# A hybrid mLSTM, window and neighbourhood attention step on one core: the final norm's path to the output, and the place of two instructions in the attention schedules

## What is computed

```python
def _rmsnorm(x, w):
    xf = x.astype(jnp.float32)
    y = xf * lax.rsqrt(jnp.mean(xf * xf, axis=-1, keepdims=True) + NORM_EPS)
    return (y * w.astype(jnp.float32)).astype(x.dtype)
...
    y_prompt = _rmsnorm(xc, final_norm_w)
    y_sample = _rmsnorm(xl, final_norm_w)
```

## Time and profile before

| what | value |
|---|---|
| device time, median of 3 runs | 1920.52 us (1920.36 to 1920.54) |
| the profiled execution's own time | 1920.54 us |
| its span, first to last instruction | 1918.7 us |
| busy: PE / DVE / ACT / POOL | 1862.4 / 1269.0 / 931.1 / 270.2 us |
| mean granted TensorE clock | 0.99 of full speed |
| DMA | 412.99 MB, 215 GB/s over the span |

### The profile page before, as it was taken

The page is one execution under the profiler, slowest core; times in us unless marked ns, Lnnn a source line. Parts: engine busy times, 40 slices in busy tenths (PEclk is TensorE's granted clock), DMA queues, the critical chain, the costliest instruction groups (busy, mean ns, idle before and its releaser), DMA issues.

```text
span 1918.7 us, 32356 instructions
## 1 busy us (share of the span) xinstructions
PE 1862.4 (97%) x13828; PEld 1660.9 (87%) x13828; DVE 1269.0 (66%) x1737; ACT 931.1 (49%) x1373; POOL 270.2 (14%) x198
## 2 busy tenths in 40 slices
PE   5999999999999999999999999999999999989998
PEld 2999777798999867999977689998998777889998
DVE  3854576666786566787555678857655776658874
ACT  2753344544564354555344455645543445436552
POOL 2100121002111112111011221101100220021111
PEclk8999999999999999999999999999999999989999
DMA  9555346866655757655574775456654447634552
GB/s 369 191 224 190 139 154 241 299 230 266 233 182 194 275 214 293 242 212 198 180 303 174 289 281 217 177 199 242 227 191 154 156 173 280 247 143 176 187 187 77
DMA packets 65823, 412.99 MB, mean 215 GB/s; under 512 B 11744, under 2 KB 12048, under 8 KB 17424
## 3 DMA queue, kind: packets, MB, share of 16 engines
q1 hardware_dynamic: 54288, 392.98, 54.9%
q10 hardware_dynamic: 11392, 17.95, 2.7%
HBM read 400.10 MB, written 10.76 MB: 214 GB/s over the span
## 4 chain that ended last, share of the span: by engine, by line
PE 88%; DVE 5%; POOL 2%; ACT 2%; issue 2%; DMA 1%; POOLq 0%; DVEq 0%; ACTq 0%; SPq 0%
PE ps L537 15%; PE ps L538 14%; PE ps L539 14%; PE ps L554 9%; PE ps L588 6%; PE ps L590 6%; PE ps L589 6%; PE ps L570 4%; PE ps L601 3%; PE ps L821 1%; DMA raw<-in_stream 1%; DVE spl_lo L454 1%; PE ps L805 1%; POOL hf L2192 1%; ACT Ea L1365 1%
## 5 line engine op out<-in xcount | busy, mean ns | idle before, releaser
L454 DVE TENSOR_TENSOR spl_lo<-raw,spl_hi 128x1024 fp32r<-128x1024 f32 x556 | 727.9, 1341 | 266.6 <-ACT spl_hi L443 265.8
L443 ACT ACTIVATE spl_hi<-raw 128x1024 fp32r<-128x1024 f32 x556 | 566.6, 1054 | 310.6 <-PE ps L590 163.2
L537 PE MATMUL ps<-H_hi,spl_hi 128*128 128x256 f32 x1920 | 549.4, 286 | 11.7 <-DVE H_lo L1619 10.1
L538 PE MATMUL ps<-H_lo,spl_hi 128*128 128x256 f32 x1920 | 545.4, 284 | 0.0
L539 PE MATMUL ps<-H_hi,spl_lo 128*128 128x256 f32 x1920 | 545.2, 284 | 0.0
L537 PEld LDWEIGHTS ps<-H_hi,spl_hi 128*128 128x128 f32 x1920 | 370.5, 193 | 32.3 <-issue 32.2
L538 PEld LDWEIGHTS ps<-H_lo,spl_hi 128*128 128x128 f32 x1920 | 370.7, 193 | 0.1
L539 PEld LDWEIGHTS ps<-H_hi,spl_lo 128*128 128x128 f32 x1920 | 370.6, 193 | 0.0
L588 PE MATMUL ps<-G_hi,spl_hi 128*128 128x256 f32 x704 | 199.2, 283 | 0.0
L589 PE MATMUL ps<-G_lo,spl_hi 128*128 128x256 f32 x704 | 199.2, 283 | 0.0
L590 PE MATMUL ps<-G_hi,spl_lo 128*128 128x256 f32 x704 | 199.2, 283 | 0.0
(11 more groups left out here) (241 smaller groups left out, 2778.2 us busy)
## 6 DMA issues: line engine op xcount, KB each, us to landing
raw<-in_stream SPq DMA_DIRECT2D x374, 1024.0 KB, 4.8
out_new_C<-c_stage ACTq DMA_DIRECT2D x16, 512.0 KB, 4.9
ada_b<-in_ada_b ACTq DMA_DIRECT2D x4, 768.0 KB, 8.8
x<-in_x ACTq DMA_DIRECT2D x1, 1024.0 KB, 12.1
cache<-in_na_cache ACTq DMA_DIRECT2D x1, 1024.0 KB, 8.9
bias<-in_rpb ACTq DMA_DIRECT2D x1, 1024.0 KB, 13.4
small<-in_small ACTq DMA_DIRECT2D x1, 838.5 KB, 7.6
cache<-in_swa_cache ACTq DMA_DIRECT2D x1, 512.0 KB, 8.0
```

Source lines behind the costliest of these rows:

```text
L443: act.activation(spl_hi[m % SPL][:, :], raw[r % RAW][:, h * HALF:(h + 1) * HALF], ACT.Copy).then_inc(S["hi_done"], 1)
L454: dve.tensor_tensor(spl_lo[m % SPL][:, :], raw[r % RAW][:, h * HALF:(h + 1) * HALF], spl_hi[m % SPL][:, :].bitcast(F32), ALU.subtract).the ...
L537: pe.matmul(out, w_hi, x_hi, start=st, stop=False, skip_group_check=True)
L538: pe.matmul(out, w_hi, x_lo, start=False, stop=False, skip_group_check=True)
```

## The change

Three edits.

1. The end: `norm(2 * DEPTH)` is now called on PE, so the sums are followed by `roots`. DVE makes four quarters of the normalised result in `yT` with `normal`, PE transposes them into `ACC[0..3]`, ACT copies quarters 0 and 2 and DVE quarters 1 and 3 to `yrow` (one 128x512 copy each), and ACT issues all four output DMAs, two after quarters 0 and 1 and two after quarters 2 and 3. SP issues none.
2. swa, on ACT: `exps(3)` comes ahead of the copy of `queries(1)`.
3. na, on DVE: `split("qkv", i, 1, 1, 0)` comes ahead of `reciprocals(1)`.

```diff
@@ tensor
+            norm(2 * DEPTH)
             for g in range(4):
-                if g == 3:
-                    square_sums(2 * DEPTH)
-                pe.wait_ge(S["xa_done"], g + 1)
+                pe.wait_ge(S["hm_done"], 4 * 2 * DEPTH + g + 1)
                 for s in range(NS):
                     for c in range(2):
                         k = 2 * g + c
-                        mm = pe.transpose(ROWS[g][:, s * TOK + c * P:s * TOK + (c + 1) * P],
-                                          xa[:, k * TOK + s * T:k * TOK + (s + 1) * T], ident)
+                        mm = pe.transpose(ACC[g][:, s * TOK + c * P:s * TOK + (c + 1) * P],
+                                          yT[:, k * TOK + s * T:k * TOK + (s + 1) * T], ident)
                 mm.then_inc(S["yt_mm"], 1)
@@ scalar, swa
                     attended(0)
+                    exps(3)
                     queries(1, ACC[0])
-                    exps(3)
                     weights(2)
@@ scalar, end
-            act.wait_ge(S["rstd_done"], 2 * DEPTH + 1)
-            for s in range(NS):
-                for g in range(2):
-                    act.wait_ge(S["yt_mm"], g + 1)
-                    act.activation(y_columns(s, g), ROWS[g][:, s * TOK:(s + 1) * TOK], ACT.Identity,
-                                   scale=rstd[:, s:s + 1]).then_inc(S["yrow_a"], 1)
-            act.wait_ge(S["yrow_a"], 4)
-            act.dma_start(io["y_sample"][0, :, 0:512], yrow[:, D:D + 512]).then_inc(S["y_landed"], 16)
+            for g in (0, 2):
+                act.wait_ge(S["yt_mm"], g + 1)
+                copy(y_columns(g), v3(ACC[g][:, :], TOK), "yrow_a")
+                act.wait_ge(S["yrow_a"], g // 2 + 1)
+                act.wait_ge(S["yrow_d"], g // 2 + 1)
+                for s, y in enumerate(("y_prompt", "y_sample")):
+                    o = g * TOK
+                    act.dma_start(io[y][0, :, o:o + 512], yrow[:, s * D + o:s * D + o + 512]).then_inc(S["y_landed"], 16)
@@ vector, na
                     maxima(1)
+                    split("qkv", i, 1, 1, 0)
                     reciprocals(1)
-                    split("qkv", i, 1, 1, 0)
                     used("qkv", i, 0, 1, 1)
@@ vector, end
-            dve.wait_ge(S["rstd_done"], 2 * DEPTH + 1)
-            for s in range(NS):
-                for g in range(2, 4):
-                    dve.wait_ge(S["yt_mm"], g + 1)
-                    dve.tensor_scalar(y_columns(s, g), ROWS[g][:, s * TOK:(s + 1) * TOK], rstd[:, s:s + 1], None,
-                                      ALU.mult).then_inc(S["yrow_d"], 1)
+            inverse_rms(2 * DEPTH)
+            for g in range(4):
+                normal(yT[:, g * 512:(g + 1) * 512], xa, g).then_inc(S["hm_done"], 1)
+            for g in (1, 3):
+                dve.wait_ge(S["yt_mm"], g + 1)
+                dve.tensor_copy(y_columns(g), v3(ACC[g][:, :], TOK)).then_inc(S["yrow_d"], 1)
```

More of the change, by code:

```diff
@@ L356, in build @@
     bias = sb("bias", NH * T, F32, rX + 8 * KB)
+    yT = sb("yT", KD * TOK, F32, rA)
     yrow = sb("yrow", NS * D, F32, rA + 8 * KB)
@@ L398, in build @@
     SCORES = (UP[1], MISC)
-    ROWS = (UP[0], UP[1], ADA_PS, ACC[0])
     def sc(name, k=0, n=1, rows=P, r0=0):
@@ L422, in build @@
         s_mm nm_done exp_done esink_in esink_done rsum_done pn_done pt_mm pt_a pt_d o_mm o_hi o_lo
-        xa_done yt_mm yrow_a yrow_d y_landed""".split()
+        yt_mm yrow_a yrow_d y_landed""".split()
     S = {n: nc.alloc_semaphore(n) for n in names}
@@ L481, in state_queries, with y_columns @@
         return t if d is None else t[:, :, d, :]
-    def y_columns(s, g):
-        return yrow[:, s * D + g * TOK:s * D + (g + 1) * TOK]
+    def y_columns(g):
+        return v3(yrow[:, :], D)[:, :, g * TOK:(g + 1) * TOK]
     class Link:
@@ L511, in _ @@
                 sp.dma_start(raw[n % RAW][:, :], io["stream"][n]).then_inc(raw_landed[n % RAW], 16)
[L512 to L517, removed]
         @block.tensor
@@ L1576, in mod_columns, with scaled @@
                                                   nw.unsqueeze(2).to_broadcast([P, KD, 2]), ALU.add, ALU.mult))
-            def scaled(pair, last):
+            def scaled(pair):
                 o = slice(pair * 512, (pair + 1) * 512)
@@ L1582, in scaled @@
                 link.wait()
[L1583 to L1588, removed]
+                link(dve.tensor_tensor(v3(xa[:, o], T), v3(x[:, o], T), coef_a[:, co].unsqueeze(2).to_broadcast([P, 4, T]),
+                                       ALU.mult))
             def residual(r, pair):
@@ L1645, in project @@
                         residual(r, pair)
-                        scaled(pair, r == 2 * DEPTH - 1)
+                        scaled(pair)
             def splits(n0, count):
@@ L2148, in _ @@
                 ffn(i)
-            dve.wait_ge(S["ssq_mm"], 2 * DEPTH + 1)
-            dve.tensor_scalar(var[:, :], MISC[:, 0:NS], 1.0, D * EPS, ALU.mult, ALU.add).then_inc(S["xvar_done"], 1)
-            dve.wait_ge(S["rstd_done"], 2 * DEPTH + 1)
-            for s in range(NS):
-                for g in range(2, 4):
-                    dve.wait_ge(S["yt_mm"], g + 1)
-                    dve.tensor_scalar(y_columns(s, g), ROWS[g][:, s * TOK:(s + 1) * TOK], rstd[:, s:s + 1], None,
-                                      ALU.mult).then_inc(S["yrow_d"], 1)
+            inverse_rms(2 * DEPTH)
[4 more added lines that the diff above has]
+                dve.tensor_copy(y_columns(g), v3(ACC[g][:, :], TOK)).then_inc(S["yrow_d"], 1)
         @block.gpsimd
```

## The result

The changed kernel took 1931.64 us (median of 5, 1928.54 to 1932.46), the kernel before beside it 1920.54: a ratio of 1.0054 with an interval of 1.0043 to 1.0066, so 8 to 13 us slower. The forecast was 1927.4, and 1930.2 the upper end of its range: the direction was right and the size too small. By means the difference is +9.4 (standard error 1.0). The result lists 14 executions of the changed kernel in all, from 1928.54 to 1935.24 with a mean of 1931.7. The profiled one took 1930.35, its span is 1928.6, and it is 9.8 above the profiled execution before (1920.54).

What follows compares the result with a forecast made beforehand. PE was taken to bound the kernel (88% of the chain of waits). End 3.9 + swa 0.1 + na stall 2.5 + clock 0.4 = +6.9 us on the median of 1920.52, so 1927.4; range 1923.9 to 1930.2, 8 in 10.

Steps and rivals of the forecast that it cites:

- The end: End of the kernel: the new path with paired ACT issues costs +3.9, low end +3.1, high +4.8.
- the 0.2 that I gave it for the transposes: End: with transposes at full clock, DVE's quarter 1 is copied 0.2 sooner.
- Stall 2.5 and clock 1.65: na: PE's dense work starts 2.5 late, then 3.3 us of work at half speed costs 1.65 more.
- The clock term: PE clock in na and later: 1.65 lost, half of 2.5 returned; +0.4, from -1.3 to +2.9.
- the two losses further on may move or vanish: Half-clock stretches from 1073.90 and at handoff 1100, worth 2.5, may change when everything shifts by 4 us; half counted returned.
- The handoff at 649: Handoff similar to that at 1100, but at full clock; taken as evidence that such work comes out both ways.
- the 1.6 for the stretch behind 1073.90: After na's edit: 3.70 us at 0.54 of the clock, taken as worth about 1.6.
- the 0.48 on PE: swa: scores(4) starts 0.48 later on PE; hidden since nm ends with POOL's multiply, otherwise the edit costs 0.48.
- the term of 0.1: swa: the edit delays exps(4) by +0.1, with 0 and +0.5 as ends.
- The clock does not pay back: Rival on PE's clock: all of 1.65 stands or more, +8.2 to +9.4, 1929; chance 0.2.
- Pays back: Rival on PE's clock: new half-speed stretch 1.65, both later stretches gone (-2.5); +5.3, 1925.8; chance 0.3.
- Caught downstream: Rival on na: some later wait ended last anyway and absorbs the stall; +4, 1924.5; chance 0.07.

Runs made afterwards that it cites:

- e7: Kernel before with the new end alone, its four output DMAs issued by SP instead of ACT; ran once, 1925.59 us, end 4.00 longer than before.
- e11: Changed kernel with extra transposes that compute nothing filling PE's gaps in swa (12), na (34) and end (6, 8, 8); mean +8.5 (± 0.7) over the kernel before.
- e8: Kernel before with the new end alone, DMAs issued by SP, 6, 8 and 8 filler transposes on PE; ran once, 1922.51 us, end 2.83 longer.
- e4: Kernel before with the na edit alone and 34 filler transposes on PE ahead of weights(1); mean +3.2 (± 0.6).
- e3: Kernel before with the swa edit alone; mean +2.5 (± 0.7), ratio 1.0014 (1.0004 to 1.0023).
- e6: Kernel before with filler transposes in four PE gaps (swa, na at 1072 us, handoff q = 7, ahead of first mLSTM products); mean +0.1 (± 0.9).
- e12: Kernel before with the end's sums ahead of transposes of quarter 2 instead of 3, and fillers around q = 7 alone; mean -2.6 (± 0.8), ratio 0.9987.
- e5: Kernel before with the swa edit and 12 filler transposes on PE ahead of scores(4); mean +1.9 (± 0.6), ratio 1.0006 (0.9997 to 1.0015).
- e10: Changed kernel run again, unaltered, beside e9; mean +9.3 (± 0.8) over the kernel before, ratio 1.0047 (1.0034 to 1.0060).
- e9: Changed kernel with the swa edit undone, end and na edits kept; mean +9.4 (± 1.0) over the kernel before, ratio 1.0045 (1.0032 to 1.0059).
- e2: Kernel before with the na edit alone; mean +4.6 (± 0.6), ratio 1.0023 (1.0014 to 1.0032).

## Why the prediction was wrong, and where it was right

**The end: right.** Laid out at +3.9; the traces with this end have 4.04, 3.33, 4.00, 4.02 and 3.52, mean 3.8. The order of waits was as told. ACT's copy of quarter 2 stood behind its two issues and was done at 1925.18; DVE's copy of quarter 3 stood behind the half-clock transposes and was done last, at 1925.31, so that taking the issues off ACT gained nothing (e7). The lower clock's part is larger than the 0.2 that I gave it for the transposes: 1.0 with ACT's issues (e11), and 0.15 more once SP issues and ACT is free (e8). With the clock up the end costs 2.98, just below the low end of 3.1.

**na: right.** Stall 2.5 and clock 1.65, together 4.15; measured 4.04, 4.03, 4.05 and 4.58 in the four traces that have the edit without filler. e4 and e11 separate the parts, 2.5 and 1.5. The Trainium skill (TensorE: Matmul & The Clock Gate, HAM oscillation) warned of this restart, and the traces agree, with 3.4 us at the lower level behind 4.27 idle.

**The clock term: the step that failed.** I took +0.4 for it, 1.65 less half of 2.5, because "the two losses further on may move or vanish". They stayed in all four traces with the na edit and no filler (a clock of 0.5 behind 1075 and behind 1103 in each), and the stages around them did not get shorter: the rest of na was +0.63, -0.02, +0.04 and -0.04, and the stage with the second mLSTM, which I had not counted among the places at risk, was +1.75, -0.01, +1.98 and +0.04. The two reasons behind the term fail as well. The handoff at 649 kept the clock and the one at 1100 lost it in all 14 traces, so these were two different places and not one place drawn twice. And the 1.6 for the stretch behind 1073.90 was priced as if nothing but PE ended the next wait: in the two traces where that stretch is missing, e3 and e6, PE waited 1.66 and 1.89 for a transfer instead, and the rest of na was longer, not shorter.

Three stages vary between traces in just two or three lengths: to swa 595.5 or 593.9, second mLSTM 374.0 or 375.6 to 377.2, around q = 7 61.1 or 59.6 to 60.0 (59.1 with fillers). So the trace of before was itself one draw, slow in two of these and fast in one. A draw that an edit shifts has no reason to come back better than the mean; the term for the later stretches should have been 0 with a width of some 3 us to each side (my estimate from these lengths). The forecast would then have been 3.9 + 0.1 + 2.5 + 1.65 = 8.15 above 1920.54, 1928.7.

In the profiled execution this step is the whole miss. That execution is 9.8 above before, the forecast was 6.9; the end, na and swa together came within 0.3 of their terms, and the stages without an edit, forecast at -1.25, came out at +1.9 (0.8 of it at the start). The median of the five lies another 1.3 above that execution, and this part is spread that I cannot place; the mended sum of 8.15 is 1.2 below the difference of the means, +9.4.

That clock levels go with these lengths is read from the traces. The six traces with a long second mLSTM have a stretch at 0.50 in it and the other eight have none; the same holds to swa, behind 200, for ten traces and four. Around q = 7 the level lasts 10.2 us in the six traces with 61.1, 6.8 in the six with 59.6 to 60.0, and is absent in e6 and e12. That the level makes the length is tested by fillers at q = 7 alone. The start has no such steps: it varies from 62.98 to 66.19, and I did not find out why. These windows are of the changed kernel, behind 1104, in the second mLSTM, and at q = 7:

```profile
1106.00:1109.50 3.50, 3.50 (x16) 0.51 1.01 424
1474.70:1478.10 3.40, 3.40 (x10) 0.50 0.82 267
...
1723.90:1727.30 3.40, 3.40 (x17) 0.50 0.00 0
```

**swa: the cost right, one consequence missed.** `exps(4)` moved by the 0.1 that was laid out. Not quite as told, `nm` no longer waited for POOL; the maxima ended just as POOL did. Where the clock held the stage was -0.16, +0.05 and +0.15 (the changed kernel, e5, e11), beside +0.1; without the edit it varies by 0.5 too. But the edit lengthens PE's idle time from 1.41 to 1.9, and in e3 and e10 the clock fell behind it, +1.77 and +2.07. I costed the 0.48 on PE as hidden by POOL and did not ask what a longer idle time does there, though I asked it in na. How often it falls stays open: behind this gap it fell in two of the three traces that have the edit and no filler, and in none of the nine without the edit. Two of those nine have a longer stage as well (+0.77 in e4 and +3.16 in e6), but there the clock fell at 700, ahead of the gap. By the means the edit is worth 2.5 (± 0.7) alone and, in the whole change against e9, about 0 (± 1.2). So the term of 0.1 may be too small by as much as 2.4 on the mean; the runs do not settle it.

**The rivals.** "The clock does not pay back", 1929 at a chance of 0.2, came nearest. "Pays back" had 0.3 and was not seen. "Caught downstream" fell with e2, where nothing came back behind na. The trouble with "pays back" was not only its chance: e3 shows that a vanished stretch need not pay.

**The range.** It ended at 1930.2, with +2.2 for the clock as its upper reach. I built it on the profiled execution and three runs within 0.2 us. The kernel's own executions later spread over 8.

## What to carry to other kernels

On an engine that runs its list in order, an instruction that only releases others (here `reciprocals(1)`, 0.18 us) belongs ahead of long work, even when that work looks more urgent: putting it behind cost 2.5 us here and 1.5 more for the matmuls that restarted at 1.2 GHz. Every change that lengthens TensorE's idle time wants its own question, what the clock does behind it, and three equal times are no measure of a kernel's spread. Where a gap cannot be closed, fillers that compute nothing kept the clock up in na, at the end and at q = 7; try them place by place, since the set of four at once gained nothing. And before a stretch at half clock is counted as time to be won, look for the wait behind it: here TensorE ran into a wait of 1.7 us for a transfer instead.

## What the runs showed of the hardware

Executions of one kernel on one core spread from 1916.2 to 1924.0 (34 of the kernel before), and traces differ in which stretches have the granted clock at 0.5; in three stages the lengths go with it. After an idle time of 1.9 us in swa the level fell in two traces (e3, e10) and held in one, the changed kernel's; after 4.3 us in na the clock was down in all four traces that have that gap unfilled (the changed kernel, e2, e9, e10). After 1.97 us in the rest of na it fell in all 13 traces that have that gap, but for e3.

A VectorE instruction with one SBUF input of 128x4 also took longer beside GpSimd: `nm` in na, shown above, took 0.72 from 1019.52 and ended just after POOL's multiply at 1020.22, where 0.17 is usual. The Trainium skill (GPSIMD Engine Reference, Key points) names instructions in a 2-port mode beside those with two inputs; this is consistent with it, though no run here shows the mode.
